# The inverse's rounds in a recurrence: half as many columns, and each round's first product run together with the second product of the round before

## The reference, cut to what matters

```
def step(s, inp):
    r_t, w_t, k_t, v_t, kk_t, b_t = inp
    sa = einsum('bhij,bhj->bhi', s, kk_t)
    s = s * w_t[:, :, None, :] - sa[..., None] * b_t[:, :, None, :] + v_t[..., None] * k_t[:, :, None, :]
    return s, einsum('bhij,bhj->bhi', s, r_t)
```

## Time and profile before

| | |
|---|---|
| median of 3 runs | 3060.09 us |
| the profiled execution's own time | 3051.25 us |
| its span | 3049.4 us |
| TensorE busy | 2768.1 us, 91% |
| VectorE busy | 1873.5 us, 61% |
| ScalarE busy | 1167.6 us, 38% |
| GpSimd busy | 1027.6 us, 34% |
| the 12 passes and the last stage | 2024.65 to 2527 us of the span |

### The profile page before, as it was taken

The page is one execution under the profiler, slowest core; times in us unless marked ns, Lnnn a source line. Parts: engine busy times, 40 slices in busy tenths (PEclk is TensorE's granted clock), DMA queues, the critical chain, the costliest instruction groups (busy, mean ns, idle before and its releaser), DMA issues. The chain is left out here.

```text
span 3049.4 us, 59055 instructions
## 1 busy us (share of the span) xinstructions
PE 2768.1 (91%) x24960; PEld 2191.1 (72%) x24960; DVE 1873.5 (61%) x2795; ACT 1167.6 (38%) x2168; POOL 1027.6 (34%) x576
## 2 busy tenths in 40 slices
PE   7998898999989988989999799978888887799987
PEld 5775576878867655767788587857777775579875
DVE  5998656887059996478860555547777744363062
ACT  4634434333246344243331422235444533332252
POOL 1432142545424311324454122235555530033202
PEclk9999999999999999999999899989999988899988
DMA  6331133433333211244333332320000004142211
GB/s 226 91 84 49 43 90 99 145 118 94 100 86 101 71 44 50 83 130 147 114 96 95 101 106 88 97 66 19 25 24 24 25 9 152 35 118 77 66 29 56
DMA packets 350230, 249.36 MB, mean 82 GB/s; under 512 B 10874, under 2 KB 322448, under 8 KB 349456
## 3 DMA queue, kind: packets, MB, share of 16 engines
q1 hardware_dynamic: 342704, 229.56, 25.0%
q10 hardware_dynamic: 7264, 16.03, 1.7%
HBM read 221.52 MB, written 16.52 MB: 78 GB/s over the span
## 5 line engine op out<-in xcount | busy, mean ns | idle before, releaser
L545 POOL TENSOR_TENSOR weights_lo<-weights_raw,weights_hi 128x1024 fp32r<-128x1024 f32 (+1 forms) x214 | 546.5, 2555 | 1008.9 <-ACT weights_hi L514 1008.9
L1188 PE MATMUL psum<-moving_hi,weights_hi 128*128 128x512 f32 x1344 | 542.6, 404 | 34.7 <-PEq L173 13.7
L1188 PE MATMUL psum<-moving_lo,weights_hi 128*128 128x512 f32 x1344 | 530.0, 394 | 0.0
L1188 PE MATMUL psum<-moving_hi,weights_lo 128*128 128x512 f32 x1344 | 529.4, 394 | 0.0
L1188 PEld LDWEIGHTS psum<-moving_hi,weights_hi 128*128 128x128 f32 x1344 | 255.8, 190 | 143.1 <-issue 60.0
L514 ACT ACTIVATE weights_hi<-weights_raw 128x1024 fp32r<-128x1024 f32 (+1 forms) x218 | 226.3, 1038 | 227.5 <-PE psum L1188 227.5
L1188 PEld LDWEIGHTS psum<-moving_hi,weights_lo 128*128 128x128 f32 x1344 | 256.0, 190 | 55.2
L1188 PEld LDWEIGHTS psum<-moving_lo,weights_hi 128*128 128x128 f32 x1344 | 256.6, 191 | 47.7
L2630 POOL TENSOR_TENSOR second_off<-second_mats,second_masks 128x256 f32<-128x256 f32 x180 | 150.1, 839 | 108.6 <-PE psum L2087 107.7
L545 POOL TENSOR_TENSOR odd_lo<-odd_raw,odd_hi 128x2048 fp32r<-128x2048 f32 x16 | 74.4, 4649 | 318.8 <-ACT odd_hi L514 318.8
L2686 PE MATMUL psum<-hn_hi,even_hi 128*128 128x256 f32 x480 | 166.1, 346 | 7.3 <-DVE hn_lo L2023 7.3
(11 more groups left out here) (473 smaller groups left out, 6430.3 us busy)
## 6 DMA issues: line engine op xcount, KB each, us to landing
weights_raw<-in_w_up SPq DMA_DIRECT2D x88, 512.0 KB, 3.7
weights_raw<-in_w_in SPq DMA_DIRECT2D x80, 512.0 KB, 3.6
ada<-in_ada_w SPq DMA_DIRECT2D x9, 2048.0 KB, 8.9
odd_raw<-in_od_w_in SPq DMA_DIRECT2D x16, 1024.0 KB, 5.6
even_raw<-in_ev_w_in SPq DMA_DIRECT2D x30, 512.0 KB, 4.0
weights_raw<-in_w_down SPq DMA_DIRECT2D x32, 448.0 KB, 3.6
weights_raw<-in_w_o SPq DMA_DIRECT2D x16, 512.0 KB, 3.9
weights_raw<-in_w_down SPq DMA_DIRECT2D x16, 512.0 KB, 3.8
```

Of the source, the lines that this page charges most:

```text
L545: ops.tensor_tensor(self.ring.lo[i % n][:, a:b], self.ring.raw[:, t % self.ring.landing, a:b], self.ring.hi[i % n][:, a:b].bitcast(F32), A ...
L1188: return nc.tensor.matmul(to, (hi, lo)[which][:, at:at + P], moving(k)[part], start=start and k == 0 and i == 0, stop=stop and k == n_k - ...
```

## The change

- The first product takes only the columns that a level fills. Below the last level these are every other block of `wb`, 32 of 64 columns; at the last level it still takes 64. The second product makes 32 columns in every round. Where it made 64 it now makes, at the last level, the half of the transpose that is missing.
- The first product is crossed, so it uses the two corners of the array that a straight product leaves free. ScalarE copies it in two activations of 64 partitions each, which bring the halves back.
- TensorE issues the first product of round n and the second of round n - 1 together, chunk by chunk, in two parts of two chunks. All waits of both stand ahead of the first part. Slot 2n and the phase lie between the parts, slot 2n + 1 after the second.
- ScalarE's copy moves behind the steps of slot 2n. VectorE adds 32 columns instead of 64.

```
-            bank_y, bank_w = lambda n: bank(n % 2, CH), lambda n: bank(2 + n % 2, CH)
+            half = CH // 2
+            bank_y = lambda n, level: bank(n % 2, half if level < last_level else CH)
+            bank_w = lambda n: bank(2 + n % 2, half)
+            def blocks(x, level, odd):
+                return x.rearrange("p c (b two l) -> p c b two l", two=2, l=LEVELS[level])[:, :, :, odd, :]
+            def y_at(g, level):
+                return y[:, own(g), 0:half if level < last_level else CH]
...
+                    def make_y(n, c):
+                        level, g = rounds[n]
+                        begun = buf.wb[:, slots(g), CH:]
+                        begun = blocks(begun, level, d) if level < last_level else begun
+                        return halves_matmul(nc, bank_y(n, level)[:, c, :], off[:, n % 2, c, :], begun[:, c], crossed=True)
+                    def make_w(n, c):
+                        level, g = rounds[n]
+                        wt, y_ = buf.wb[:, slots(g).start + c, 0:CH], y_at(g, level)[:, c, :]
+                        if level == last_level:
+                            wt, y_ = y_, wt[:, half * (1 - d):half * (1 - d) + half]
+                        return halves_matmul(nc, bank_w(n + 1)[:, c, :], wt, y_)
...
                             if n >= 2:
                                 pe.wait_ge(y_taken, n - 1)
-                            for c in range(4):
-                                last = halves_matmul(nc, bank_y(n)[:, c, :], off[:, n % 2, c, :], buf.wb[:, slots(g).start + c, CH:])
-                            last.then_inc(y_ready, 1)
-                        steps(len(units) + 2 * n)
-                        beside(UNIT_PLACES + n)
                         if n:
...
-                            for c in range(4):
-                                wt, y_ = buf.wb[:, s0 + c, 0:CH], y[:, own(g).start + c, :]
-                                last = halves_matmul(nc, bank_w(n)[:, c, :], *((wt, y_) if level < last_level else (y_, wt)))
-                            last.then_inc(w_ready, 1)
-                        steps(len(units) + 2 * n + 1)
+                        for part in range(2):
+                            for c in range(2 * part, 2 * part + 2):
+                                if n < len(rounds):
+                                    last_y = make_y(n, c)
+                                if n:
+                                    last_w = make_w(n - 1, c)
+                            if part and n < len(rounds):
+                                last_y.then_inc(y_ready, 1)
+                            if part and n:
+                                last_w.then_inc(w_ready, 1)
+                            steps(len(units) + 2 * n + part)
+                            if not part:
+                                beside(UNIT_PLACES + n)
... (ScalarE)
+                        steps(len(units) + 2 * n)
                         if n < len(rounds):
                             level, g = rounds[n]
                             act.wait_ge(y_ready, n + 1)
-                            S.activation(y[:, own(g), :], bank_y(n), ACT.Identity).then_inc(y_taken, 1)
-                        steps(len(units) + 2 * n)
+                            for hf in range(2):
+                                to, at = slice(64 * hf, 64 * hf + 64), slice(64 - 64 * hf, 128 - 64 * hf)
+                                last = S.activation(y_at(g, level)[to], bank_y(n, level)[at], ACT.Identity)
+                            last.then_inc(y_taken, 1)
... (VectorE)
+                            if level < last_level:
+                                w_ = blocks(buf.wb[:, slots(g), CH:], level, d)
+                            else:
+                                w_ = blocks(buf.wb[:, slots(g), 0:CH], level, 1 - d)
+                            made = bank_w(n).rearrange("p c (b l) -> p c b l", l=LEVELS[level])
+                            V.tensor_tensor(w_, w_, made, ALU.add).then_inc(w_added, 1)
```

More of the change, by code:

```diff
@@ L2530, in _ @@
                                 pe.wait_ge(y_taken, n - 1)
-                            for c in range(4):
-                                last = halves_matmul(nc, bank_y(n)[:, c, :], off[:, n % 2, c, :], buf.wb[:, slots(g).start + c, CH:])
-                            last.then_inc(y_ready, 1)
-                        steps(len(units) + 2 * n)
-                        beside(UNIT_PLACES + n)
                         if n:
                             level, g = rounds[n - 1]
-                            s0 = slots(g).start
                             pe.wait_ge(y_taken, n)
@@ L2619, in _ @@
                             dve.wait_ge(w_ready, n)
-                            w_ = buf.wb[:, slots(g), CH:] if level < last_level else buf.wb[:, slots(g), 0:CH]
-                            V.tensor_tensor(w_, w_, bank_w(n), ALU.add).then_inc(w_added, 1)
+                            if level < last_level:
[4 more added lines that the diff above has]
+                            V.tensor_tensor(w_, w_, made, ALU.add).then_inc(w_added, 1)
                         steps(len(units) + 2 * n + 1)
```

## The result

The kernel after takes 3220.57 us (median of 4 runs, 3215.59 to 3223.54), beside 3059.36 us for the kernel before in the same job (4 runs, 3057.24 to 3064.57): a ratio of 1.0526, 95% interval [1.0512, 1.0541]. It is 161 us slower. Slower was forecast, with 8.7 us; the time lies 120 us above the range. The profiled execution has a span of 3217.7 us against 3049.4.

The account below looks back on a forecast made before the run. The prediction took the recurrence chain, interleaved with product filler, as the bound. Pass 0 +1.6, five odd passes +0.45 each, five even +1.05 each and pass 11 -0.4 gave +8.7 us on 3060.1: 3069 us, range 3042 to 3100.

Parts of the forecast that it names:

- the bound is the chain: Rounds: dependent recurrence steps across engines, 2.04 us a chunk, 1.2 to 1.3 us an iteration, with products as filler.
- four matmul instructions, one in each corner: TensorE products: four in 58.4 ns, both products 0.467 us instead of 0.934, removing 6.5 us of issue a pass.
- no gain from 32 columns on TensorE: TensorE products: weights keep 64 columns and their load sets the pace, so halving the moving columns saves nothing.
- the addition at 0.27 us: VectorE's addition: falls from 0.398 to about 0.28 us with nobody waiting, worth 0 to -0.1 us a pass.
- the piece from the first matmul to the next copy: Step-free iteration: from TensorE's first matmul to the start of ScalarE's next copy, forecast at 0.67 us.
- the copy on the path: Joined iteration waits for ScalarE's previous copy: a step-free iteration becomes 1.17 us from 0.93, 1.40 at the last level.
- back 0.05: Step-free iteration: return from the end of ScalarE's copy to TensorE's next matmul, put at 0.05 us.
- the copy: ScalarE's copy as two overlapping activations: 0.45 us against 0.38, bounds 0.28 to 0.55; last level 0.66.
- The walk: Sixteen iterations of each pass kind stepped through in engine order: pass 0 +1.6, even +1.05, odd +0.45, pass 11 -0.4 us.
- Rival C: TensorE's clock falls to 1.2 GHz in half the rounds of 11 passes: 36 us more, 3105 us; chance 0.20.
- steps go on between, and the units ahead are dense: Argument against a clock fall in the rounds: recurrence steps continue and dense units precede each pass.
- What would show it: Trace signs: right if `second_y` releases most iterations; wrong if 16 instructions take 0.12 us, rounds 1.4 or less, clock 0.5.

Follow-up runs that it names:

- experiment 2: Changed kernel plus one 256-column matmul on constants, result unused, behind each iteration's products: 3169.87 us, ratio 1.0362.
- experiment 6: Kernel before, old order, with 32-column copy, second product and addition, but the first product keeping 64 columns: 3050.53 us, ratio 0.9988.
- 7: Kernel of experiment 6, old order kept, with the first product in crossed corners and its copy as two activations: 3079.6 us, ratio 1.0069.
- 5: Changed kernel with the wait for ScalarE's copy last, doubled waits dropped, and a 256-column filler matmul in each pause: 3161.71 us, ratio 1.0354.
- experiment 4: Kernel before, with its straight corners, order and waits, plus the change's 32-column slices: 3072.35 us, ratio 1.0061.
- experiment 8: Changed kernel, joined order and its waits, with the first product in straight corners and one activation as copy: 3224.42 us, ratio 1.0537.

## Why the prediction was wrong

**Right**: that the bound is the chain and not TensorE's issue; four matmul instructions, one in each corner, in 58 ns (32 in 0.44 to 0.47 us at full clock); no gain from 32 columns on TensorE; the addition at 0.27 us with nobody waiting; the piece from the first matmul to the next copy, 0.69 us for 0.67; and so the direction, though the forecast of +8.7 us is a small part of the 161. On the columns the prediction read the Trainium skill too short. In "TensorE: Matmul & The Clock Gate" the table of the section "Back-to-back issue gap" has one value for 1 to 64 columns, about 60 cycles, so by it too the step from 64 to 32 saves nothing. The trace agrees (0.66 us for sixteen with 32 columns, 0.63 with 64).

**The step that failed at full clock is "the copy on the path", in its term "back 0.05".** That figure came from a step's answer, whose matmul waits for one thing. The whole iteration has up to six waits at its head, and I read them in the diff as conditions that are met, not as instructions that TensorE must still pass once the late one is through. Forecast at 0.05, it is 0.36 us; in order it is 0.14. With the copy at 0.55 us (the first and last term of "the copy", 0.45, was too low, since the second activation does not begin 0.10 us before the first one's end; 0.55 was the far bound), a step-free iteration is 1.60 us, 0.43 more than forecast, which over 14 iterations is 6 us a pass. Part of that stands beside steps and phases: by experiment 2 the rounds at full clock, fillers included, grow by 5.3 us in pass 0, 5.9 in an even pass, 6.7 in an odd one and 7.1 in pass 11, where I had 1.6, 1.05, 0.45 and -0.4. The walk also had the order of passes wrong: pass 0 should have grown most and even ones more than odd ones, and at full clock pass 0 grew least and odd ones more than even.

The walk was also held against the wrong edge. The 28.75 and 29.45 us of passes 6 and 7 end with the addition to `second_o`, 0.7 us behind the inverse's last one, where pass 11 and its walk end. Up to that one the even passes before took 27.9 us and the odd ones 28.7 on average. If the walk's 29.8 and 29.9 end there too, it gave +1.9 and +1.2 a pass, some +17 us in all and not +8.7: still far below what came.

How the 75 us split, as a chain of edits at full clock: narrow products and copies -9 (experiment 6 against before), the crossed copy +21 (7 against 6), the joined order with its waits in order +52 (5 against 7), the waits' own order +11 (2 against 5). The +52 is what remains of the 75, and it holds the fillers' own cost. Most likely it is the joined wait itself: no product lies between the steps any more while ScalarE works. But the order also moved ScalarE's copy behind a step, and the phase ahead of the second part, and no run took these one by one.

**Rival C is the other half, and was priced too low.** It had a chance of 0.20 and 36 us; the clock took 70 us in the rounds and about 14 in the units (experiment 2). I had the clock fall in half the rounds of 11 passes and charged only the chain's slower chunk, 0.66 us, five times a pass: 3.3 us. The weights' load, which I had just found to set the pace, slows down with the clock, from 58 ns for four instructions to 104 (32 of them spread over 0.44 and over 0.78 us). The same instructions at 0.57 took 12.3 us longer (experiment 4). "TensorE: Matmul & The Clock Gate" in the Trainium skill gives in "LDWEIGHTS (loading the stationary operand)" a load's time by its columns alone, which for 64 columns makes an estimate of 53 ns; at full clock the trace comes near (58 ns from one load to the next in a corner), at half clock it does not (104). And the fall was not half of the rounds' time: mean clocks of 0.52 to 0.70, between levels of 0.5 and 1, are half clock in 60 to 96% of it, 81% over all passes. Of "for it" and "against" in that rival, "steps go on between, and the units ahead are dense" was no defence: the last 5.6 us of pass 0's units ran at 1.00 (2036 to 2041.62), the first 4.4 us of its rounds at 0.64 and the next 6 at 0.50; it had come back to full clock by the iteration shown above, behind the matmuls of a phase, and was at half again in the next.

"What would show it" named three signs of error; the third, a granted clock of 0.5 between 2036 and 2490 us, is what the profile shows. The idle rows did not name `second_y` in most iterations, but that was a fault of the sign: they name what ended last.

**What stays open**: what decides in which passes the clock falls. Fillers held it in even passes and lost odd ones; joined and straight showed the same pattern, at lower clocks; and in experiment 2 the units kept full clock even behind a pass at half, which they had not in the change. Nor is it known why 5 us of the units' growth stay at full clock.

## What to carry to other kernels

When an edit moves a wait from one small operation to the head of a block, list every wait that the block passes, put the one that comes last at the end of the list, and price the return with all of them. Where the engine's pace is set by weight loads, columns that cost nothing may help to keep its clock up, as experiments 4 and 6 suggest: before you take work off TensorE, price a stretch at half clock with everything on it doubled, weight loads too. Of an engine that serves as filler between a chain's steps, issue time is not free to give away: here 78 us of issue went, and the rounds grew by up to 75 us even at full clock.

## What the runs showed of the hardware

- A wait instruction on TensorE that is already met, behind one that was late, costs 0.11 us: the late one with two behind it makes 0.36 us from the copy's end to the matmul, the late one last 0.14, and a step's single wait 0.05 to its weight load.
- Two activations of 64x128 from PSUM take 0.55 us, two of 64x256 0.77, one of 128x128 0.28: halving the partitions saves nothing, and they don't overlap.
- With the clock at half, a weight-bound product of 32 instructions in four corners is spread over 0.78 us and not 0.44, and a pass's rounds at 0.57 took 39.81 us where the same instructions at 1.00 took 27.55.
- The profile's busy share does not tell which rounds keep the clock. Of the rounds of pass 0, those of experiment 2 held 1.00 at 21.76 us busy of 26.92 (81%) and those of experiment 6 at 17.45 of 20.86 (84%); those of experiment 8 fell to 0.52 at 31.49 of 38.61 (82%) and those of experiment 4 to 0.86 at 20.38 of 23.70 (86%). At half clock the same work looks busier.
